# Attention in a hybrid encoder layer: spreading the reciprocal softmax totals over the partitions, by TensorE transposes or by a store and a load through DRAM

## The reference

```
h = rmsnorm(x, norm_g); z = h @ w_in
out_A = mla(c_q, c_kv, k_rope)      # 4 heads, latent attention, width 512
out_B = pool_mixer(u)               # centred mean pooling, width 256
out_C = gla(q, k, v, gates)         # gated linear attention, both directions, width 256
mixed = concat(out_A * silu(gate), out_B * silu(gate), out_C * silu(gate))
y = rmsnorm(x + mixed @ w_out, final_norm_g)
```

```
s = q_nope . k_nope + q_rope . k_rope
p = softmax(s * scale); o = p @ v
```

## Time and profile before

| | |
|---|---|
| median of 3 runs | 846.65 us |
| profiled execution, its own time | 847.75 us |
| its span, first to last instruction | 846.0 us |
| mean granted TensorE clock | 0.97 |
| attention, from barrier to barrier | 452 to 691.3 us of the span |
| PE busy in attention (452 to 691.3) | 224.4 us |
| DVE busy there | 149.2 us |
| ACT busy there | 110.7 us |
| DMA share there | 0.11 |

### The profile page before, as it was taken

The page is one execution under the profiler, slowest core; times in us unless marked ns, Lnnn a source line. Parts: engine busy times, 40 slices in busy tenths (PEclk is TensorE's granted clock), DMA queues, the critical chain, the costliest instruction groups (busy, mean ns, idle before and its releaser), DMA issues. The chain is left out here.

```text
span 846.0 us, 14631 instructions
## 1 busy us (share of the span) xinstructions
PE 767.9 (91%) x6092; PEld 644.0 (76%) x6092; DVE 416.4 (49%) x704; ACT 330.1 (39%) x574; POOL 195.1 (23%) x222
## 2 busy tenths in 40 slices
PE   5999999999999997999935899999999957999996
PEld 4896868787888876888824788788888845788885
DVE  3654776365555420144422566666666747433332
ACT  4441644344554422233111544444544553233321
POOL 2323126363464310324000000000000016233320
PEclk9999999999999998999976999999999987999999
DMA  6312021011112133211231000000033022555541
GB/s 237 123 51 69 26 86 50 27 40 65 51 40 77 64 114 137 55 58 44 58 128 63 13 14 14 13 26 13 14 112 138 1 68 82 173 175 174 174 136 50
DMA packets 39324, 64.53 MB, mean 76 GB/s; under 512 B 3520, under 2 KB 22368, under 8 KB 39264
## 3 DMA queue, kind: packets, MB, share of 16 engines
q1 hardware_dynamic: 33264, 49.51, 18.3%
q10 hardware_dynamic: 6000, 14.16, 4.5%
HBM read 44.00 MB, written 19.27 MB: 75 GB/s over the span
## 5 line engine op out<-in xcount | busy, mean ns | idle before, releaser
L77 PE MATMUL psum<-h_hi,z_w_hi 128*128 128x512 f32 (+1 forms) x480 | 184.5, 384 | 0.4 <-POOL z_w_lo L797 0.4
L79 PE MATMUL psum<-h_hi,z_w_lo 128*128 128x512 f32 (+1 forms) x480 | 178.5, 372 | 0.0
L78 PE MATMUL psum<-h_lo,z_w_hi 128*128 128x512 f32 (+1 forms) x480 | 178.1, 371 | 0.0
L77 PEld LDWEIGHTS psum<-h_hi,z_w_hi 128*128 128x128 f32 x480 | 91.8, 191 | 18.6 <-issue 2.2
L79 PEld LDWEIGHTS psum<-h_hi,z_w_lo 128*128 128x128 f32 x480 | 91.5, 191 | 16.2 <-issue 0.4
L78 PEld LDWEIGHTS psum<-h_lo,z_w_hi 128*128 128x128 f32 x480 | 91.8, 191 | 14.7 <-issue 0.7
L1672 ACT ACTIVATE a_weights<-psum,a_bias,mla_q_scale 128x1024 f32<-128x1024 f32 (+1 forms) x48 | 51.1, 1065 | 103.7 <-DVE a_bias L1711 103.7
L77 PE MATMUL psum<-o_w_hi,o_m_hi 128*128 128x512 f32 x192 | 76.3, 398 | 13.9 <-DVE o_w_lo L2009 13.3
L1890 POOL TENSOR_TENSOR mla_mixed<-mla_mixed,o_gate_first 128x512 f32 (+1 forms) x6 | 7.7, 1286 | 317.1 <-ACT o_gate_first L1925 317.1
L78 PE MATMUL psum<-o_w_lo,o_m_hi 128*128 128x512 f32 x192 | 75.7, 394 | 0.0
L79 PE MATMUL psum<-o_w_hi,o_m_lo 128*128 128x512 f32 x192 | 75.7, 394 | 0.0
(11 more groups left out here) (216 smaller groups left out, 1455.3 us busy)
## 6 DMA issues: line engine op xcount, KB each, us to landing
z_w_raw<-in_w_z_dram SPq DMA_DIRECT2D x17, 512.0 KB, 3.5
n_x_in<-in_x_dram SPq DMA_DIRECT2D x12, 512.0 KB, 3.8
gates_scratch<-z_gate ACTq DMA_DIRECT2D x24, 256.0 KB, 2.1
o_x_in<-in_x_dram SPq DMA_DIRECT2D x12, 512.0 KB, 3.6
out_dram<-o_y ACTq DMA_DIRECT2D x12, 512.0 KB, 3.0
o_w_raw<-in_w_out_dram SPq DMA_DIRECT2D x8, 512.0 KB, 9.1
rope_scratch<-p_rope_split SPq DMA_DIRECT2D x12, 256.0 KB
a_q_rope<-rope_scratch SPq DMA_DIRECT2D x12, 256.0 KB, 2.6
```

What stands on the lines that cost most here:

```text
L77: nc.tensor.matmul(out, a_hi, b_hi, start=first, stop=False)
L78: nc.tensor.matmul(out, a_hi, b_lo, start=False, stop=False)
L79: return nc.tensor.matmul(out, a_lo, b_hi, start=False, stop=last)
```

## The change

The reciprocals of pair p are spread by SP: when both are there, SP stores the two columns (128 x 2) to a scratch tensor in DRAM, waits until they have landed, and loads the 256 values back to all 128 partitions as `share_row`. TensorE's two transposes and DVE's copy are gone. The multiplication waits for this load too and reads the row with a stride, since the stored values alternate between the two tiles of the pair. SP's loop is written over the step m, and so the ninth load of `q_rope` and the loads of output weights stand among these transfers. Outside attention two pairs of semaphores are merged into one each, with waits on higher counts of the same events.

```diff
-            def invert_means(of, ready, step):
-                pool.wait_ge(ready, 1)
-                nc.gpsimd.tensor_scalar(of[:, :], of[:, :], EPS, None, ALU.add).then_inc(step, 1)
-                pool.wait_ge(step, 1)
+            def invert_means(of, n):
+                pool.wait_ge(mean_ready, n + 1)
+                nc.gpsimd.tensor_scalar(of[:, :], of[:, :], EPS, None, ALU.add).then_inc(root_step, 1)
+                pool.wait_ge(root_step, 2 * n + 1)
...
+            def load_output_weights():
+                sp.dma_start(keep.gate_first[:, :, :], gates_dram[:, :, 0:P].rearrange("a p t -> p a t")).then_inc(gate_loaded, 16)
+                sp.dma_start(keep.mix_first[:, :, :], mix_dram[:, :, 0:P].rearrange("a p t -> p a t")).then_inc(mix_loaded, 16)
+                sp.wait_ge(turned, QUERY_END[HEADS - 1, TB - 1])
+                for k in range(KT):
+                    sp.dma_start(keep.w_out[k][:, :], w_out_dram[k * P:(k + 1) * P, :]).then_inc(w_out_loaded[k], 16)
+
+            def spread_share(p):
+                sp.wait_ge(share_ready, 2 * p + 2)
+                sp.dma_start(share_dram[p, :, :], share[:, 2 * p:2 * p + 2]).then_inc(share_stored, 16)
+                sp.wait_ge(share_stored, 16 * (p + 1))
+                if p >= 2:
+                    sp.wait_ge(gathered, p - 1)
+                sp.dma_start(share_row[:, p % 2, :], share_dram[p, :, :].rearrange("q n -> (q n)").partition_broadcast(P))\
+                  .then_inc(share_spread, 16)
+
             for b in range(TB):
                 load_rope(0, b)
-            for h in range(HEADS):
-                for b in range(TB):
-                    if (h, b) == (HEADS - 1, 1):
...
-                        sp.wait_ge(turned, QUERY_END[HEADS - 1, TB - 1])
-                        for k in range(KT):
-                            sp.dma_start(keep.w_out[k][:, :], w_out_dram[k * P:(k + 1) * P, :]).then_inc(w_out_loaded[k], 16)
-                    if h + 1 < HEADS:
-                        sp.wait_ge(scores_done, TILES * h + 4 * b + 4)
-                        load_rope(h + 1, b)
+            for m in range(1, STEPS + GATHER_LAG):
+                if m % 4 == 0 and m <= STEPS - TILES:
+                    h, b = (m - 4) // TILES, (m - 4) % TILES // 4
+                    sp.wait_ge(scores_done, m)
+                    load_rope(h + 1, b)
+                if m == STEPS - 8:
+                    load_output_weights()
+                for p in pair_at(m, TURN_LAG):
+                    spread_share(p)
...
                     dve.wait_ge(output_done, p + 1)
-                    nc.vector.tensor_copy(share_row[:, p % 2, :], psum[:, 6 + p % 2, PAIR:]).then_inc(share_copied, 1)
-                    dve.wait_ge(share_copied, p + 1)
-                    nc.vector.tensor_tensor(keep.mixed[:, h, t:t + PAIR], psum[:, 6 + p % 2, :PAIR],
-                                            share_row[:, p % 2, :], ALU.mult).then_inc(gathered, 1)
+                    dve.wait_ge(share_spread, 16 * (p + 1))
+                    nc.vector.tensor_tensor(keep.mixed[:, h, t:t + PAIR].rearrange("p (n q) -> p n q", n=2),
+                                            psum[:, 6 + p % 2, :PAIR].rearrange("p (n q) -> p n q", n=2),
+                                            share_row[:, p % 2, :].rearrange("p (q n) -> p n q", n=2), ALU.mult).then_inc(gathered, 1)
...
-                pe.wait_ge(share_ready, 2 * p + 2)
                 pe.wait_ge(latent_lo_ready, p + 1)
-                for n in range(2):
-                    nc.tensor.transpose(psum[:, 6 + p % 2, PAIR + n * P:PAIR + (n + 1) * P],
-                                        share[:, 2 * p + n:2 * p + n + 1].broadcast_to([P, P]), ident[:, :])
```

More of the change, by code:

```diff
@@ L281, in phase_front @@
         cq_lo_ready = sem("p_cq_lo_ready")
-        kv_mean_ready = sem("p_kv_mean_ready")
-        kv_root_step = sem("p_kv_root_step")
+        mean_ready = sem("p_mean_ready")
+        root_step = sem("p_root_step")
         kv_rows_ready = sem("p_kv_rows_ready")
@@ L538, in take_kv_mean @@
                 act.wait_ge(sq_mm, TB)
-                nc.scalar.activation(mean_sq[:, :], psum[:, 3, 0:TILES], ACT.Copy).then_inc(kv_mean_ready, 1)
+                nc.scalar.activation(mean_sq[:, :], psum[:, 3, 0:TILES], ACT.Copy).then_inc(mean_ready, 1)
             def fill_kv_rows():
-                act.wait_ge(kv_root_step, 2)
+                act.wait_ge(root_step, 2)
                 act.wait_ge(w_v_lo_ready, 1)
@@ L564, in take_q_mean @@
                 act.wait_ge(sq_mm, SQUARES)
-                nc.scalar.activation(rstd[:, :], psum[:, 7, 0:TILES], ACT.Copy).then_inc(q_mean_ready, 1)
+                nc.scalar.activation(rstd[:, :], psum[:, 7, 0:TILES], ACT.Copy).then_inc(mean_ready, 1)
             def take_w_rope():
@@ L889, in subtract @@
                 return nc.gpsimd.tensor_tensor(out, whole, high.bitcast(F32), ALU.subtract)
-            def invert_means(of, ready, step):
-                pool.wait_ge(ready, 1)
-                nc.gpsimd.tensor_scalar(of[:, :], of[:, :], EPS, None, ALU.add).then_inc(step, 1)
-                pool.wait_ge(step, 1)
-                nc.gpsimd.tensor_tensor(of[:, :], of[:, :], minus_half[:, :].broadcast_to([P, TILES]), ALU.pow).then_inc(step, 1)
+            def invert_means(of, n):
+                pool.wait_ge(mean_ready, n + 1)
+                nc.gpsimd.tensor_scalar(of[:, :], of[:, :], EPS, None, ALU.add).then_inc(root_step, 1)
+                pool.wait_ge(root_step, 2 * n + 1)
+                nc.gpsimd.tensor_tensor(of[:, :], of[:, :], minus_half[:, :].broadcast_to([P, TILES]), ALU.pow)\
+                  .then_inc(root_step, 1)
             pool.wait_ge(biased, 2 * TB)
@@ L905, in _ @@
             split_lo(15)
-            invert_means(mean_sq, kv_mean_ready, kv_root_step)
+            invert_means(mean_sq, 0)
             split_lo(16)
@@ L912, in _ @@
             subtract(keep.k_rope_lo[0:ROPE, :], k_swapped[:, :], keep.k_rope[0:ROPE, :]).then_inc(k_rope_lo, 1)
-            invert_means(rstd, q_mean_ready, q_root_step)
-            pool.wait_ge(q_root_step, 2)
-            nc.gpsimd.tensor_scalar(keep.q_scale[:, :], rstd[:, :], MLA_SCALE, None, ALU.mult).then_inc(q_root_step, 1)
+            invert_means(rstd, 1)
+            pool.wait_ge(root_step, 4)
+            nc.gpsimd.tensor_scalar(keep.q_scale[:, :], rstd[:, :], MLA_SCALE, None, ALU.mult).then_inc(root_step, 1)
             pool.wait_ge(w_rope_hi_ready, 1)
@@ L1624, in phase_mla_attend @@
         output_done = sem("a_output_done")
-        share_copied = sem("a_share_copied")
+        share_stored = sem("a_share_stored")
+        share_spread = sem("a_share_spread")
         gathered = sem("a_gathered")
```

13 lines of the change are left out of this document (4 added, 9 removed).

## The result

| | before | after |
|---|---|---|
| median of 5 runs (range) | 846.93 us (846.35 to 848.32) | 852.88 us (850.82 to 856.99) |
| ratio, 95% interval | | 1.0069 [1.0049, 1.0088] |
| profiled execution: its own time, its span | 847.75, 846.0 | 851.07, 849.3 |
| of the span: ahead of attention | 452.8 | 450.9 |
| attention, to SP's first issue of the output block | 238.5 | 243.7 |

The change makes the kernel 5.9 us slower, outside the range of 844.0 to 848.5. In the profiled executions attention is 5.2 us longer, and the block behind it takes what it took. (The stretch ahead of attention ends between 450.7 and 454.6 us in the 14 profiled executions here, and is left out of the comparison.)

What follows compares the result with a forecast made beforehand. Attention was taken as bound in turn by PE's work and the chain DVE, ACT, DVE. Body -0.9 and end +0.1 make -0.8 us: 846.95 for the profiled execution, 845.8 us as the median's forecast; range 844.0 to 848.5.

Steps and rivals of the forecast that it cites:

- Two loops take turns: Attention: PE's own work and the chain DVE, ACT, DVE alternate as the bound, so few of PE's savings count.
- TensorE leads everywhere: Rival: all 5.3 us that PE loses in attention shorten the kernel, to 841.5 us; chance 0.13.
- The body gives 0.9 us: Fewer transposes gain 0.7 us at step 10 of heads 0 to 2, 0.2 at step 40; 19 other places nothing.
- only lengthen that wait: Odd steps: dropping DVE's 24 copies, 0.42 us each, just lengthens its wait for ACT; nothing in the body.
- the trip is 5.0 us, between 4.1 and 6.1: SP's store and load through DRAM: 2.1 us store, 2.6 load, 0.3 for three hand-overs.
- Pair 23 … 0.1 us later: End of attention: the row lands at 690.70, so the last multiplication ends at 691.12, 0.1 us later than before.
- Pair 19 … 2.7 us are left: nothing: Behind the output weights on SP's queue, its row lands at 671.3, needed by 674.0, so no cost.
- The weights themselves … nothing: Output weights, loaded later, are still there some 24 us before the next block starts; no cost.
- the merged semaphores: nothing: Outside attention: merged semaphores count the same events in the same order, so no change.
- the trip is long: Rival: an 8 us trip adds 2.15 us at pair 19 and 3.1 at the end, 851.0 us; chance 0.12.

Runs made afterwards that it cites:

- no_spread: Kernel before without the 48 transposes and 24 copies, nothing in their place, multiplying by a row of ones (division left out): 845.87 us, ratio 0.9983.
- double_turns: Kernel before with each pair's two transposes of reciprocals made twice, 96 in all: 848.84 us, ratio 1.0023.
- plain_load: weights_pieces with the share row loaded from 128 different DRAM rows, not one row 128 times (division left out): 848.43 us, a single execution.
- weights_pieces: Changed kernel with gates and mix issued sooner and output weights loaded as one 512 KB piece per step, steps 37 to 44: 852.05 us, ratio 1.0059.
- weights_late: Kernel before with gates, mix and output weights held back until pair 19's reciprocals are there: 847.50 us, ratio 0.9999.
- sems_only: Kernel before with only the merged semaphores ahead of attention: 847.64 us, ratio 1.0010.
- hybrid19: Changed kernel, weights as in the change, but pairs 19 to 23 spread by transposes and copy as before: 848.46 us, ratio 1.0006.
- hybrid21_pieces: weights_pieces with pairs 21 to 23 spread by transposes and copy as before: 847.58 us, ratio 1.0006.

## Why the prediction was wrong, step by step

- **What bounds attention: right.** Two loops take turns. "TensorE leads everywhere", the rival with -5.3 us, was refuted from both sides (no_spread -1.4, double_turns +1.5). From head to head it is 57.60 us now (tile 23 to 35, 112.66 to 170.26), where I had 57.5. By the rule of the Trainium skill, *Perfetto Trace Analysis*, section "Identifying the Most-Contended Engine", PE's work was the work to cut; this case's runs bear it out only in part, since cutting 5.3 us of it gave 1.4.
- **"The body gives 0.9 us": right to tile 41.** no_spread gave 0.88 there, double_turns cost 0.96, the changed kernel gained 0.72 and 0.80. Missed: steps 42 to 46, the short tiles, give another 0.44.
- **The copies "only lengthen that wait": right** as far as no_spread's sum shows. They weren't tried alone.
- **"I take 2.1 … I take 2.6 … the trip is 5.0 us, between 4.1 and 6.1": this step failed.** The medians of store and load are 2.9 + 4.0 = 6.9 us, without hand-overs, and the last pair's trip took 8.5 to 9.8 on SP's queue. For the store I took the row of a large contiguous one, short by 0.8. For the load I took a row of the right bytes (2.7 in plain_load, so that row was right for *distinct* addresses) and had only said, in a rival, that 128 reads of one row are in no row. The load from the one row just written takes 1.3 us more. Both ends of my bound were ends for another kind of transfer. The sentence that rows of up to 256 KB without large transfers ahead are all under 3 us was a misreading besides: `p_w_rope`, 256 KB at 392.23 us with nothing issued on the queue for 20 us before, landed after 3.2. The estimate from the Trainium skill, *DMA: Bandwidth & Descriptors*, section "Anatomy of one DMA — SWDGE (gpsimd) path", 4.3 us for the two, is 2.6 short of the 6.9 too.
- **"Pair 23 … 0.1 us later": failed by 3.5.** Besides the trip's size, I gave pair 23 an empty queue. Pair 22's load is issued 0.4 us ahead of its store in the changed kernel, which took 5.4 us, and 0.8 in weights_pieces, where it took 4.5. weights_pieces has this part alone, with a tail of +3.6.
- **"Pair 19 … 2.7 us are left: nothing": failed.** I had the weights end at 666.5 and the row there at 671.3, in the time of before. Mine was a landing of the store at 668.6, which is 666.1 in the time of this execution (its reciprocals of pair 19 come 2.5 us sooner, 654.96 against 657.47); it landed at 667.77, 1.7 later. The weights started later than my 651.0: pair 18's store took 2.85 us and not 2.1, and the gates' issue behind its load 2.40 and not 0.45. Then three things came that I hadn't priced: the load was 4.0; SP, which waits for each landing, started pair 20 3.5 us late; and from then on each store was issued within a microsecond of the load ahead of it. Stalls of 1.35 and 1.69 us in the body cost 0.7 to 0.9 at tile 47 (216.46 against 215.78 of weights_pieces and 215.59 of no_spread), and the tail is 2.1 us longer than that of weights_pieces.
- **"The weights themselves … nothing", "the merged semaphores: nothing": right** (weights_late 0.9999, sems_only 1.0010).
- **The rival "the trip is long"** had the mechanism, both places and nearly the size (851.0), at 0.12. It put 2.15 us on pair 19 and 3.1 more on the end. The profiles show 0.9 in the body and 5.7 in the tail, since late pairs hand their delay on through one queue, which the rival didn't have. It took a trip of 8 us for every pair; by its own working, 2.9 and 4.0 give an estimate of +1.7 us in all. That its sum came near 852.9 is in part luck.

In the profile the sum is: body -1.3 (no_spread's), stalls +0.9, tail +5.7 against before, together +5.3. Attention measured +5.2, the medians +5.9 and +5.1.

## What to carry to other kernels

In this kernel a round trip through DRAM is covered where its result is wanted more than 10 us later, and exposed at the end of the block, where nothing covers it. There the old way is better, and keeping it for the last pairs took the loss away. Price such a trip with rows of the same kind (piece size, repeated or distinct source, whether the source was just written, what was issued just ahead on the queue), and where no row is of that kind, let the range say so. And when a small urgent transfer shares a queue with large ones, and the issuing engine waits for its landing, count the delay of every later transfer on that queue too, not only of the first.

## What the hardware showed that I had not expected

- **Loading one row, just written, into all partitions is slow.** 128 KB as 128 reads of the same 1 KB take 4.0 us, from 128 rows 2.7, in the median. Loads issued right behind are slower as well: `a_q_rope` 4.2 us against 2.6 in the earlier trace rows, and 3.0 in plain_load.
- **Queue or engines.** A 1 KB store took 2.4 to 2.6 us at best, 4.3 to 5.7 right behind one such load, 10.9 to 12.8 behind 4.75 MB. Whether the queue's order or the engines' work does it stays open: on another queue a 1 KB store took 2.6 us, but not under the same conditions. One window of the changed kernel speaks against the engines' being busy all the time (columns as in the earlier trace rows):

```profile
684.25:685.75 1.50, 1.41 (x12) 1.21 (x11) 0.00 (x0) 0.05 (x1) 0.00 (x0) 1.00 0.00 0
```

Pair 22's load (issued at 683.75) and pair 23's store (684.11) are both under way, and for these 1.5 us the profile has no traffic on the DMA engines.
- **The output block has two lengths.** It takes 154.5 to 154.7 us in some profiled executions and 156.1 to 156.6 in others, the changed kernel with its same instructions once 154.7 and once 156.3. The granted clock tells them apart, 20 to 30 us behind the block's start; here the changed kernel, its first profile and its second (busy of PE, PEld, DVE, ACT, POOL; then PEclk, DMA share, GB/s):

```profile
714.60:724.60 10.00, 10.00 (x46) 8.26 (x45) 2.59 (x4) 2.11 (x3) 3.19 (x3) 1.00 0.12 32
```

```profile
714.83:724.83 10.00, 10.00 (x39) 8.03 (x38) 2.59 (x4) 2.10 (x3) 3.20 (x3) 0.84 0.00 1
```

PE is busy 0.3 of the block's first 10 us in both, at a granted clock of 0.50. In the window shown one is at 2.4 GHz throughout, the other, with 0.84, at 1.2 GHz for part of it. The difference of 1.6 us is as large as the whole gain of a free spreading. That hybrid19 and hybrid21_pieces have a shorter attention and not a shorter time may be this (their profiled executions had the long block), but with one profile of each this stays open, as does the 1.7 us of weights_pieces.
